# Strassen pooling in a decoder step: weight sums kept in DRAM for the second half of the tokens, operand rows and sample work handled later

## The reference, cut to what matters

```python
u, z = split(rmsnorm(x) @ w_in)             # 1024 -> 2 x 2048
mix  = trailing_mean(u, windows 2/4/8/16 per channel group) - u
mix  = einsum(mix, w_map per group) * scale
x    = x + (mix * silu(z)) @ w_out
```

## Time and profile before

| | us |
|---|---|
| runs shown, lowest / median / highest of 3 | 2909.94 / 2913.86 / 5648.6 |
| profiled execution, device time | 2909.62 |
| profiled execution, span | 2907.9 |
| head of the pooling layer | 0 to 154.3 |
| units 0 to 31 | 154.3 to 844.6 |
| PE busy over the span | 2798.3 (96%) |

### The profile page before, as it was taken

How to read it: one execution, slowest core, us unless ns; L and a number is a source line. 1 busy time by engine, 2 the same in 40 slices (tenths; PEclk the granted TensorE clock), 3 DMA queues, 4 the chain that set the end, 5 groups by cost and what they waited for, 6 DMA issues and landing times. The chain is left out here.

```text
span 2907.9 us, 45393 instructions
## 1 busy us (share of the span) xinstructions
PE 2798.3 (96%) x16738; PEld 2329.8 (80%) x16738; DVE 1924.0 (66%) x2858; ACT 1420.8 (49%) x2313; POOL 449.2 (15%) x370
## 2 busy tenths in 40 slices
PE   8998989899999999999999999999999999999998
PEld 7776768787877888888888888879999999865787
DVE  3466777878863232477667666588888888754654
ACT  5554434433332221455646454367777777733322
POOL 1223434355510000000000000100000000012321
PEclk9999999999999999999999999999999999999999
DMA  8743323445346766487988878873444444599543
GB/s 280 234 158 98 124 89 139 143 149 167 118 162 224 235 209 211 180 293 267 302 276 267 271 257 257 260 166 80 111 101 108 108 101 102 196 382 415 204 177 109
DMA packets 329991, 562.01 MB, mean 193 GB/s; under 512 B 25545, under 2 KB 237113, under 8 KB 307385
## 3 DMA queue, kind: packets, MB, share of 16 engines
q1 hardware_dynamic: 327745, 559.24, 59.6%
q0 software_dynamic: 2048, 0.14, 0.0%
HBM read 404.90 MB, written 155.12 MB: 193 GB/s over the span
## 5 line engine op out<-in xcount | busy, mean ns | idle before, releaser
L1278 PE MATMUL pool_acc<-at_pool_x_hi,at_pool_w_hi 128*128 128x512 f32 x896 | 357.3, 399 | 46.5 <-DVE at_pool_ext L1041 27.0
L1279 PE MATMUL pool_acc<-at_pool_x_lo,at_pool_w_hi 128*128 128x512 f32 x896 | 352.6, 394 | 0.0
L1280 PE MATMUL pool_acc<-at_pool_x_hi,at_pool_w_lo 128*128 128x512 f32 x896 | 352.4, 393 | 0.0
L2715 ACT ACTIVATE attn_scores<-attn_scores,attn_lowest 128x1024 f32<-128x1024 f32 (+15 forms) x256 | 306.7, 1202 | 0.0
L2776 DVE CUSTOM_DVE_ANT_0 attn_scores<-attn_s,region_early 128x1024 f32<-128x1024 f32 (+7 forms) x256 | 216.5, 856 | 67.9 <-PE attn_s L2654 37.8
L1278 PEld LDWEIGHTS pool_acc<-at_pool_x_hi,at_pool_w_hi 128*128 128x128 f32 x896 | 170.9, 191 | 89.7 <-issue 53.6
L289 PE MATMUL outa_acc<-outa_w_hi,outa_g_hi 128*128 128x512 f32 x512 | 201.2, 393 | 6.7 <-DVE outa_w_lo L1644 4.0
L290 PE MATMUL outa_acc<-outa_w_lo,outa_g_hi 128*128 128x512 f32 x512 | 199.9, 390 | 0.0
L1280 PEld LDWEIGHTS pool_acc<-at_pool_x_hi,at_pool_w_lo 128*128 128x128 f32 x896 | 170.4, 190 | 36.6
L291 PE MATMUL outa_acc<-outa_w_hi,outa_g_lo 128*128 128x512 f32 x512 | 199.7, 390 | 0.0
L1279 PEld LDWEIGHTS pool_acc<-at_pool_x_lo,at_pool_w_hi 128*128 128x128 f32 x896 | 170.9, 191 | 34.4
(11 more groups left out here) (391 smaller groups left out, 6801.2 us busy)
## 6 DMA issues: line engine op xcount, KB each, us to landing
region_early<-w_fold SPq DMA_DIRECT2D x110, 1024.0 KB, 6.5
region_early<-in_cache_v SPq DMA_DIRECT2D x44, 512.0 KB, 7.9
hold_kq<-in_cache_k SPq DMA_DIRECT2D x40, 512.0 KB, 7.6
w_fold<-region_early SPq DMA_DIRECT2D x22, 896.0 KB, 5.9
at_pool_raw<-w_mix SPq DMA_DIRECT2D x16, 1024.0 KB, 5.5
at_pool_raw<-in_w_in_a SPq DMA_DIRECT2D x16, 1024.0 KB, 5.4
gatedT<-at_pool_z SPq DMA_DIRECT2D x32, 512.0 KB, 2.6
region_early<-gatedT SPq DMA_DIRECT2D x16, 1024.0 KB, 5.6
```

The costliest lines, as they stand in the source:

```text
L1278: pe.matmul(bank[i], a, c, start=first, stop=False, skip_group_check=begun)
L1279: pe.matmul(bank[i], a, d, start=False, stop=False, skip_group_check=begun)
L1280: x = pe.matmul(bank[i], b, c, start=False, stop=end, skip_group_check=begun)
L2715: act.activation(part, part, ACT.Exp, scale=-1.0, bias=low[s][:, x:x + 1], accum_out=sums[s][:, i:i + 1]).then_inc(expd, 1)
```

## The change

The second half uses the same weight sums as the first. The kernel now keeps all four sums of a unit in a tile of its own for each (four slots), stores the 1 MB of them to DRAM in units 0 to 15 and loads them in two halves for units 16 to 31, where POOL makes none. POOL's first sum of unit n waits until the store of unit n - 1 is complete.

Besides, steps move: the sample map from k = 6, 7 to k = 7 and the next step (in the last group it stays); the norm steps on ACT from products 3, 5 and 2 of the next unit to 5, 0 of the next and 4 of the next; on DVE from 4, 6 to 6 and 1 of the next; PE's turn from after product 0 to after product 2; the pooling steps leave slot 4 free; the load of a norm block goes ahead of the stores of the gated rows on SP; and the row operands (pieces 3 to 13) are made behind ACT's PSUM copy of the same product, those of the second half up to two to three products later (piece 7 + j at products 106, 108, 110, 112, 114, 115, 117; before 106, 107, 110, 111, 112, 113, 114). A few small tiles get other addresses.

```diff
+        self.wsum = at("w_sums", 217856, [P, 4, KH, P])
+        SUM_AT = {1: 0, 3: 1, 4: 2, 5: 3}
...
-            slots = 7 if n == LAST - 1 else 9
+            slots = (0, 1, 2, 3, 5, 6) if n == LAST - 1 else (0, 1, 2, 3, 5, 6, 7, 8)
             count = 2 * pool_length(n)
-            return [k for k in range(count) if k * slots // count == i]
+            return [k for k in range(count) if slots[k * len(slots) // count] == i]
...
+        def map_step(x):
+            for g in range(NG):
+                at = g * KC + (KC - 1 if g + 1 < NG else KC - 2)
+                if x - at in (0, 1):
+                    return g, x - at
+            return None, None
...
+        def row_operand_at(q):
+            if q < 7:
+                return {0: 3, 1: 4, 3: 5, 4: 6}.get(q)
+            return {106: 7, 108: 8, 110: 9, 112: 10, 114: 11, 115: 12, 117: 13}.get(q - 7 * (VN - 16))
...
+            def store_sums(n):
+                sp.wait_ge(w_summed, 4 * n + 4)
+                sp.dma_start(D["w_sums"][n], wsum[:, :, :, :].rearrange("p i k n -> p (i k n)")).then_inc(sums_out, 16)
+            def load_sums(n, half):
+                if n == VN:
+                    sp.wait_ge(sums_out, 16 * VN)
+                sp.wait_ge(lo, 7 * (n - 1) + (4, 6)[half])
+                part = wsum[:, 2 * half:2 * half + 2, :, :].rearrange("p i k n -> p (i k n)")
+                w = 2 * KH * P
+                sp.dma_start(part, D["w_sums"][n - VN][:, half * w:(half + 1) * w]).then_inc(sums_in[half], 16)
...  # SP, per unit n
+                if n < VN:
+                    store_sums(n)
+                b = norm_block_at(n)
+                if b is not None:
+                    norm.load(sp, b)
                 if kind == "u" and n:
                     store(n - 1, 0)
                     store(n - 1, 1)
...
-                b = norm_block_at(n)
-                if b is not None:
-                    norm.load(sp, b)
                 p, r = pair_at(n - 3)
                 if r == 0:
                     store_x(p)
                 if n == VN - 1:
                     for y in (9, 10, 11):
                         load_x(y)
+                if VN <= n + 1 < NU:
+                    load_sums(n + 1, 0)
+                    load_sums(n + 1, 1)
...  # POOL
                         if n:
                             pool.wait_ge(lo, 7 * n - 3)
+                            pool.wait_ge(sums_out, 16 * n)
...
-                if n < NU:
+                if n < VN:
                     w_sums(n, range(3))
...  # ACT, w_high
+                elif n < VN:
+                    act.wait_ge(w_summed, 4 * n + {3: 1, 4: 2, 1: 3, 5: 4}[i])
                 else:
-                    act.wait_ge(w_summed, 4 * n + {3: 1, 4: 2, 1: 3, 5: 4}[i])
+                    act.wait_ge(sums_in[i // 4], 16 * (n - VN) + 16)
...  # ACT, per product
+                    y = row_operand_at(q)
+                    if y is not None:
+                        x_high(y)
...
+                    b = norm_block_at(n - 1)
+                    if b is not None and i in (0, 4):
+                        norm_step(b, {0: 1, 4: 4}[i])
                     b = norm_block_at(n)
-                    if b is not None and i in (3, 5):
-                        norm_step(b, {3: 0, 5: 1}[i])
-                    b = norm_block_at(n - 1)
-                    if b is not None and i == 2:
-                        norm_step(b, 4)
+                    if b is not None and i == 5:
+                        norm_step(b, 0)
...  # DVE, per product
+                    b = norm_block_at(n - 1)
+                    if b is not None and i == 1:
+                        norm_step(b, 1)
                     b = norm_block_at(n)
-                    if b is not None and i in (4, 6):
-                        norm_step(b, {4: 0, 6: 1}[i])
+                    if b is not None and i == 6:
+                        norm_step(b, 0)
...  # PE
-                    if b is not None and i == 0:
+                    if b is not None and i == 2:
                         norm.turn(pe, b)
```

More of the change, by code:

```diff
@@ L337, in __init__ @@
         K["carry"] = at("carry", 83456, [P, DA // P, HIST])
-        K["win"] = at("windows", 84416, [P, len(WINDOWS) * WROW])
-        K["scale"] = at("scale_a", 84768, [P, DA // P])
-        self.gain = at("gain", 84832, [P, KC])
-        self.small = at("stats", 84864, [P, 4 * 17])
-        self.head = at("head", 85152, [P, FIRST])
-        self.zsil = at("z_sample", 85216, [P, 2 * R])
-        self.sum_halves = at("sum_halves", 85504, [P, 2 * R])
-        self.zrow = at("z_rows", 85760, [P, P])
+        K["win"] = at("windows", 228096, [P, len(WINDOWS) * WROW])
+        K["scale"] = at("scale_a", 228448, [P, DA // P])
+        self.gain = at("gain", 84416, [P, KC])
+        self.small = at("stats", 84448, [P, 4 * 17])
+        self.head = at("head", 228512, [P, FIRST])
+        self.zsil = at("z_sample", 228576, [P, 2 * R])
+        self.sum_halves = at("sum_halves", 228832, [P, 2 * R])
+        self.zrow = at("z_rows", 54016, [P, P])
         K["mixed"] = at("mixed_sample", 226048, [P, DA // P, R])
@@ L467, in run @@
         fold_place = [place(t) for t in ring]
+        sums_out, sums_in = m.sem("w_sums_out"), [m.sem(f"w_sums_in{i}") for i in range(2)]
         def at(n):
@@ L481, in quadrant @@
         def quadrant(n, i):
-            if i in (1, 5):
-                return wsum[:, 1, :, :]
-            if i in (3, 4):
-                return wsum[:, {3: 0, 4: 2}[i], :, :]
+            if i in SUM_AT:
+                return wsum[:, SUM_AT[i], :, :]
             k, c = {0: (0, 0), 2: (1, 0), 6: (1, 1)}[i]
@@ L618, in on_sp @@
                     self.load_raw(sp, g + 2)
-                if k == 6 and g + 2 < NG:
+                if k == 7 and g + 2 < NG:
                     sp.wait_ge(m_made, g + 1)
@@ L714, in w_sums @@
                 b11, b12, b21, b22 = (r[:, k * KH:(k + 1) * KH, c * P:(c + 1) * P] for k in range(2) for c in range(2))
-                t1, t24, t3 = (wsum[:, i, :, :] for i in range(3))
+                t2, t1, t3, t4 = (wsum[:, i, :, :] for i in range(4))
                 for step in steps:
@@ L726, in w_sums @@
                     elif step == 2:
+                        pool.wait_ge(w_summed, 4 * n + 1)
+                        pool.tensor_tensor(t2, b22, t1, ALU.subtract).then_inc(w_summed, 1)
+                    else:
                         if n:
                             pool.wait_ge(lo, 7 * n - 1)
-                        pool.wait_ge(w_summed, 4 * n + 1)
-                        pool.tensor_tensor(t24, b22, t1, ALU.subtract).then_inc(w_summed, 1)
-                    else:
-                        pool.wait_ge(lo, 7 * n + 2)
-                        pool.tensor_tensor(t24, b21, t24, ALU.subtract).then_inc(w_summed, 1)
+                        pool.wait_ge(w_summed, 4 * n + 3)
+                        pool.tensor_tensor(t4, b21, t2, ALU.subtract).then_inc(w_summed, 1)
             for p in range(4):
@@ L785, in rows_step, with sample_map @@
                                    ).then_inc(state_copied, 1)
-                if k == 6:
+            def sample_map(x):
+                g, step = map_step(x)
+                if step == 0:
                     act.wait_ge(m_made, g + 1)
@@ L790, in rows_step @@
                     act.activation(mrow[:, :], m_bank, ACT.Copy).then_inc(m_copied, 1)
-                if k == 7:
+                if step == 1:
                     act.wait_ge(m_turned, g + 1)
@@ L901, in on_act @@
                 rows_step(g, k)
+                sample_map(x)
                 if x == LAM_AT + 1:
@@ L913, in on_act @@
                     w_high(q + 2)
-                    if n == 0 and i in (0, 1, 3, 4):
-                        x_high({0: 3, 1: 4, 3: 5, 4: 6}[i])
-                    for j in range(7):
-                        if q == 7 * (VN - 1) + j + 1 + (2 if j >= 2 else 0):
-                            x_high(7 + j)
                     if i == 0 and kind == "u" and n:
@@ L1161, in on_dve @@
                     w_low(q + 2)
-                    if n == 0 and i in (0, 1, 3, 4):
-                        x_low({0: 3, 1: 4, 3: 5, 4: 6}[i])
-                    for j in range(7):
-                        if q == 7 * (VN - 1) + j + 1 + (2 if j >= 2 else 0):
-                            x_low(7 + j)
+                    y = row_operand_at(q)
+                    if y is not None:
+                        x_low(y)
                     if kind == "z":
```

4 lines of the change are left out of this document (2 added, 2 removed).

## The result

The changed kernel takes 2895.0 us (median of 5 runs, 2889.5 to 2896.5), the kernel before on the same chip 2910.6. The ratio is 0.9943, 95% interval [0.9927, 0.9958]: half a per cent faster, 15.6 us, where 38.7 were forecast. The interval is far narrower than the 2% that the prediction took for the limit of what can be told from no change. The time lies 2 us above the range of 2856 to 2893. One run of the kernel before took 5648.6 us and does not enter the ratio.

What follows compares the result with a forecast made beforehand. TensorE bounds the kernel (busy 2798.3 of 2907.9 us), so only its waits can be won. Terms -5.5 - 0.5 - 34.5 + 2.5 - 6.2 + 5.5 = -38.7 from 2909.6 give 2870.9; forecast 2872, range 2856 to 2893.

Steps and rivals of the forecast that it cites:

- Units 17 to 31: Second half: 6.2 us gained at product 6, 5.5 lost waiting for sums at product 1 of units 21, 23, 25, 27.
- The first part of the prediction: Bound analysis: waits also lower the granted clock, in unit 4 some 2 us on top of each long wait.
- Rival C: Units 15 on: ACT's wait for late sums makes the kernel slower, 2933 us, decisive from landings of about 9.3; chance 0.05.
- The other term: Units 17 to 31: product 6 waits go with slot 4 free and no weight sums on POOL, 6.2 us gained.
- Units 1 to 15: First half: moved norm steps and empty slot 4 remove long and product 6 waits; gain 34.5 us, ends 20 and 39.
- rival B: Units 1 to 15: norm steps give only half, pair's store lands later, DVE crowded; 14 us less, 2886; chance 0.2.
- named as a sign: Sign of being right: units 4 and 10 take 21 to 22 us.
- a sign of being wrong: Norm units: the forecast would be wrong if the square still held ACT over 8 us.
- Unit 0: First unit: ACT's PSUM copy goes first, the wait moves to products 5 and 6; gain 0.5 us, ends 0 and 4.
- Head: Before the units: moved map step removes waits of groups 1 and 2; gain 5.5 us, ends 0 (something else late) and 6.
- Unit 16: First reload unit: ACT waits for late sums, 32 us not 29.5, loss 2.5; ends gain 6 and loss 6.
- rival A: Transfers land early and unit 16 runs to its ring, gaining 6 there; -55 in all, 2855 us; chance 0.12.

Runs made afterwards that it cites:

- experiment 7: Changed kernel, but in units 18 to 31 SP waits for the first half of the sums to land before issuing the second half and what follows; 2887.5 us.
- experiment 4: Changed kernel, but the norm square's unused result goes as bf16 into a block that is not stored, so ACT skips the wait for the store; 2886.3 us.
- experiment 6: Changed kernel plus early loads of the sums, the square's free scratch block, later lambda exponentials in the head and pooling steps in nine slots; 2863.3 us.
- experiment 9: Changed kernel with only the pooling steps put back in nine slots; 2887.9 us, ratio 0.9914.
- experiment 3: Kernel before plus only the store and reload of the sums, every moved step at its old place; 2932.7 us, ratio 1.0081.
- experiment 2: Changed kernel without store and reload: POOL makes the sums in all units, the moved steps stay moved; 2880.7 us, ratio 0.9894.
- Experiment 8: Changed kernel plus early sums loads, free scratch block for the square, nine slots, unit 0's old row-operand order, lambdas' dot products at head step 14; 2857.0 us.
- experiment 1: Changed kernel with the loads of the sums issued earlier on SP, ahead of gated stores and fold, in unit 15 ahead of row pieces; 2876.0 us.

## Why the prediction was wrong

The five differences from the forecast, 13.0 + 9.1 + 2.8 + 1.9 + 0.2, make the 27 us between the forecast of -38.7 and the -11.7 that the units' end moved.

**Units 17 to 31: the step that failed most.** The place was right: the prediction named SP's hold in the fold units, the four units and product 1. Two terms of it were wrong. The landing was put at 4.4 us and was 6.7, stretched by what SP issues right behind it (experiment 7: 4.7 without, near the 4.4). And the sum held the waits alone. With 6.7 its own working gives 3.65 us for each unit, 3.25 were measured in unit 21; in all 10.9 against 5.5. The other 7.3 of the 18.2 come behind the waits, 6.9 of them behind the three that brought the clock down. The first part of the prediction had read this cost from unit 4, but here it entered only the upper end of the range and not the sum. Rival C was this mechanism with a price for it; I let it decide only from 9.3 us on and in nearly all units. It happened at less than that, as a smaller loss. The other term, -6.2 for the product 6 waits, was right: with the reload placed early the stretch is at 286.2.

By the fit of the Trainium skill (DMA: Bandwidth & Descriptors, the anatomy of one DMA), which that section states for transfers issued on the GpSimd path, 512 KB take an estimated 3.2 us. The loads of the sums are issued by SP. The trace shows 3.5 as the shortest of their 32 landings and 5.6 as their median; the fit lies below all of them, and it would have moved the sum the wrong way. All 32, in us:

```profile
DMA to landing us min/median/max: 3.5/5.6/7.5
```

The same page (queues, rings and completion order) has the engines take the descriptors of one queue in order, though a later one may finish earlier. From the order alone one might expect that followers on the same queue take nothing from a transfer ahead of them. The 6.7 against 4.7 us of experiment 7 says that they do; how, no run here shows.

**Units 1 to 15: right in its mechanism, 9.1 too much.** The long waits went as described (unit 4: 29.4 to 21.1), units 2 and 8 are at 19.9, and the forecast's wait at product 1 of units 5 and 11 is there. It was sized by PE's wait for one operand, 2 to 2.5 us, and that wait was 1.4 and 1.5. But the late square also delays the root, DVE's scaling and the turn behind it (0.6 more in unit 5, 2.0 in unit 11), so that units 5 and 11 lose 6.2 us together (experiment 4) where 4.5 were allowed. The larger miss is the slot. I gave the empty slot 4 the credit for product 6, where in fact units 1 to 15 had only one wait of a z unit, 1.51 us in unit 9; those of 0.3 lie in u units. With nine slots those waits stay away in both halves (experiments 6 and 9): in the first half the moved norm steps remove them, in the second either POOL's rest or the empty slot does (experiments 3 and 2). What the empty slot does is to push a pooling step into the stretch where POOL sums a pair. VectorE and POOL of the changed kernel at the start of unit 4:

```profile
238.16 2.28 DVE L1125 TENSOR_TENSOR at_pool_sum<-at_pool_ext 128x1038 f32<-128x1038 f32 x1
240.47 2.22 DVE L1125 TENSOR_TENSOR at_pool_sum<-at_pool_sum 128x1036 f32<-128x1036 f32 x1
...
243.21 1.17 DVE L1068 TENSOR_TENSOR at_pool_w_lo<-at_pool_w_sums,at_pool_w_hi 128x512 fp32r<-128x512 f32 x1
```

```profile
235.10 6.50 POOL L742 TENSOR_TENSOR at_pool_stage_main<-at_pool_stage_main 128x512 f32<-128x512 f32 x4 [4.21 <-ACT at_pool_stage_main L843]
```

Two adds of 2.2 us in a row, of the kind that takes 1.2 where POOL is idle, stand ahead of the operand of product 1, which then comes 1.22 late. I had a crowding of DVE in the lower end of the term and in rival B, but beside the norm's scaling, and not in the middle. With both remedies units 1 to 15 take 308.5: 34.9 less than before, where 34.5 were forecast. That the two agree is partly luck. The 4.5 us that I left standing in units 5 and 11 are gone there, and unit 10, for which I left nothing, still has waits of 1.41 and 0.93 and takes 2.9 too long. In the changed kernel it takes 23.0, over the 21 to 22 that I had named as a sign, and its square holds ACT for 8.03 us, just over the 8 that I had named as a sign of being wrong.

**Unit 0: the sign was wrong.** I said that the wait would move to products 5 and 6, and it did. ScalarE of the changed kernel, the last piece:

```profile
168.04 1.91 ACT L890 ACTIVATE at_pool_x_hi<-at_pool_x_ring 128x2048 fp32r<-128x2048 f32 x1 [5.08 <-DMA at_pool_x_ring<-x_fold]
```

The ring sets the start of product 6 in either order, 22.6 us into the unit before and 23.0 after. But PE now does its waiting in one piece of 5.18 us right ahead of it and runs it at the lower clock: 4.7 us in place of 2.8. Where the end of a chain is fixed from outside, as here, it is better that PE stands still early: the unit takes 25.4, 25.4, 25.4 and 26.0 us in the four traces with the old order and 26.8 to 27.8 in the seven with the new one.

**Head: sized too high.** The map's waits of groups 1 and 2 went. One step later DVE is late for another operand. VectorE and TensorE in the changed kernel:

```profile
74.29 1.76 DVE L1008 TENSOR_TENSOR at_pool_sum_bs<-at_pool_sum_as 128x605 f32<-128x605 f32 x1
76.08 1.17 DVE L1035 CUSTOM_DVE_ANT_0 at_pool_lambdas<-at_pool_lambdas 128x64 f32<-128x64 f32 x1
...
77.56 0.69 DVE L995 TENSOR_TENSOR at_pool_wt_lo<-pool_acc,at_pool_wt_hi 128x512 fp32r<-128x512 f32 x1
```

```profile
78.31 0.50 PE L289 MATMUL pool_acc<-at_pool_map_hi,at_pool_wt_hi 128*128 128x512 f32 x1 [2.66 <-DVE at_pool_wt_lo L995]
```

In the kernel before DVE made this operand no earlier, but PE then stood still for the map, until 80.94:

```profile
79.13 0.69 DVE L958 TENSOR_TENSOR at_pool_wt_lo<-pool_acc,at_pool_wt_hi 128x512 fp32r<-128x512 f32 x1
```

So the wait for the map had covered this one. "Something else is late by the same step" stood as an end of the range at no gain; the middle should have lain between. By the ends of the head in all traces the step is worth some 2.8 us and not 3.6. Experiment 8 removes the dots' part.

**Unit 16: right, 32.2 for 32.** ACT waited for the sums as said:

```profile
502.75 0.63 ACT L869 ACTIVATE at_pool_w_hi<-at_pool_w_sums 128x512 fp32r<-128x512 f32 x1 [9.38 <-DMA at_pool_w_sums<-w_sums]
```

Its gain of rival A's kind, 25.9, comes when the sums are early, and belongs to them and not to the row reads (25.9 against 26.3).

## What to carry to other kernels

A load put into a queue that is already held by a wait inherits that wait: place it where its buffer comes free, not where the code for it is handy, and put nothing large right behind it. A wait of TensorE can bring the clock down behind it; count that in every term (7.3 of 18.2 us here), and let what must wait do it early and in small pieces. When a step is moved away from a wait, look at what that wait had covered, and test each moved step alone: of those here the norm steps carried nearly all of the gain, the map step some 2.8 us, the row reads of unit 16 nothing, and the empty slot and the row reads of unit 0 cost.

## What the runs showed of the hardware

- Transfers issued behind one on the same queue slow it: 512 KB in 6.7 us with 2.4 MB issued within 2.5 us behind it (unit 21 of the changed kernel), 4.7 us with nothing issued behind it until it had landed (experiment 7). The same two loads of 256 KB stood ahead of it in both.
- The price of a wait grows faster than the wait. Units 21, 23, 25 and 27 of the changed kernel and of experiments 3, 4, 7 and 9 have one wait each, twenty in all. The seven of 0.8 to 1.7 us left the granted clock at the higher level and cost 0.3 us on top of themselves. The seven of 1.8 to 3.3 us behind which it fell for a shorter time cost 1.7 to 2.0 on top, and the six of 3.2 to 3.6 us behind which it fell for longer cost 2.8 to 3.2.
- The same waits can leave the clock up or bring it down: unit 11, with waits of 1.4 to 1.5 and 2.0 us, takes 25.2 us in the changed kernel and 26.7 to 26.8 in experiments 1, 2, 7 and 9, where the clock fell.
- 16 MB of extra stores, at a DMA share of 0.49 to 0.50 instead of 0.34, cost TensorE in units 1 to 15 between nothing and some 2 us (318.0, 320.6 and 320.8 against 318.4). A store that an engine waits for landed as before: in unit 4 7.8 us after its issue both with the new stores and without them (experiment 2), 8.8 in the kernel before.
